# A two-layer encoder trunk: the residual sum stays in PSUM between the stages, and the router scales after it has multiplied

## The reference

```
x = x + mixer(rmsnorm(x, g1));  x = x + hier_moe(rmsnorm(x, g2), ...)        # two layers, then rmsnorm(x, ln_f)
rmsnorm(x, g) = x * rsqrt(mean(x*x) + EPS) * g
hier_moe: g_logits = h @ w_rg + b_rg (4 groups);  g_sel = argmax;  p_g = softmax(g_logits)[g_sel]
          e_logits = (h @ w_re + b_re) of the 8 experts of group g_sel;  top_p, top_j = top_k(softmax(e_logits), 2)
          gate = p_g * top_p / sum(top_p);  out = sum over the two experts of gate * ((silu(h@w_gate) * (h@w_up)) @ w_down)
```

## Time and profile before

| | |
|---|---|
| Three runs | 1380.62, 1379.73, 1380.55 us; median 1380.55 |
| Profiled execution: its time, its span | 1383.43 us, 1381.6 us |
| Granted clock of TensorE, mean | 0.86 |
| Busy: TensorE, weight load, VectorE, ScalarE, GpSimd | 1009.7, 738.1, 349.3, 266.8, 40.5 us |
| Read from memory | 455.58 MB |

### The profile page before, as it was taken

One profiled execution on the slowest core, in us unless ns is written; L12 is line 12 of the kernel. 1 busy time (PEld: TensorE's weight loads), 2 busy tenths in 40 slices (PEclk: granted clock), 3 DMA queues, 4 the chain that ended last, 5 costly groups with the idle time before them and its releaser, 6 DMA issues.

```text
span 1381.6 us, 28941 instructions
## 1 busy us (share of the span) xinstructions
PE 1009.7 (73%) x12804; PEld 738.1 (53%) x12804; DVE 349.3 (25%) x729; ACT 266.8 (19%) x551; POOL 40.5 (3%) x74
## 2 busy tenths in 40 slices
PE   5977987766757576765799999887676666757565
PEld 2944666535435353543577778675444444544443
DVE  4355332111111111110644545431111111102011
ACT  3444221000000000000453443511000000001001
POOL 2013200000000000000000000000000000000000
PEclk9975789869988787897899999989887988879886
DMA  9630059999999999999746635469999999999994
GB/s 322 240 122 0 1 223 389 426 426 424 428 427 426 425 428 426 426 425 412 263 153 226 226 130 178 156 250 427 424 426 426 427 425 427 426 426 426 427 426 180
DMA packets 55173, 458.45 MB, mean 332 GB/s; under 512 B 4960, under 2 KB 14240, under 8 KB 30352
## 3 DMA queue, kind: packets, MB, share of 16 engines
q1 hardware_dynamic: 53936, 452.96, 79.5%
q0 software_dynamic: 1120, 3.68, 0.9%
HBM read 455.58 MB, written 1.05 MB: 331 GB/s over the span
## 4 chain that ended last, share of the span: by engine, by line
DMA 54%; PE 38%; DVE 4%; issue 2%; POOL 1%; ACT 1%; DVEq 0%; SPq 0%; PEldq 0%; POOLq 0%; ACTq 0%
DMA ring<-in_w_down 21%; DMA ring<-in_w_up 16%; DMA ring<-in_w_gate 16%; PE wk L945 6%; PE wk L633 4%; PE wk L635 4%; PE wk L634 4%; PE wk L970 3%; PE wk L620 2%; PE acc L633 2%; PE acc L635 2%; PE acc L634 2%; PE acc L812 1%; PE wk L929 1%; DMA ring<-in_w_in_e 1%
## 5 line engine op out<-in xcount | busy, mean ns | idle before, releaser
L945 PE MATMUL wk<-ring,arena 128*32 128x128 f32 x8192 | 302.4, 309 | 156.5 <-DMA ring<-in_w_up 67.9
L945 PEld LDWEIGHTS wk<-ring,arena 128*32 128x32 f32 x8192 | 259.2, 125 | 209.0 <-DMA ring<-in_w_gate 87.5
L970 PE MATMUL wk<-ring,arena 128*32 128x256 f32 x2048 | 168.9, 484 | 123.6 <-DMA ring<-in_w_down 97.9
L970 PEld LDWEIGHTS wk<-ring,arena 128*32 128x32 f32 x2048 | 74.7, 132 | 200.0 <-issue 180.8
L1640 DVE TENSOR_TENSOR arena<-wk,arena 128x128 f32<-128x128 f32 x64 | 24.0, 375 | 434.7 <-ACT arena L1277 434.7
L1651 DVE COPY arena<-wk 32x256 f32<-32x256 f32 x128 | 54.3, 424 | 229.1 <-PE wk L970 228.3
L1284 ACT ACTIVATE arena<-wk 32x256 f32<-32x256 f32 x128 | 47.7, 373 | 305.4 <-PE wk L970 304.6
L1425 DVE TENSOR_TENSOR slot_parts<-ring,slot_parts 128x1024 fp32r<-128x1024 f32 (+1 forms) x78 | 97.2, 1301 | 31.5 <-ACT slot_parts L1136 31.0
L1277 ACT ACTIVATE arena<-wk 128x128 f32<-128x128 f32 x64 | 17.7, 277 | 450.5 <-PE wk L945 450.5
L1136 ACT ACTIVATE slot_parts<-ring 128x1024 fp32r<-128x1024 f32 (+1 forms) x78 | 81.8, 1114 | 49.2 <-PEq L1068 23.2
L929 PE MATMUL wk<-arena,xn 128*128 128x128 f32 x512 | 67.8, 296 | 19.6 <-issue 10.3
(11 more groups left out here) (267 smaller groups left out, 1067.7 us busy)
## 6 DMA issues: line engine op xcount, KB each, us to landing
ring<-in_w_gate SPq DMA_DIRECT2D x64, 2048.0 KB, 35.5
ring<-in_w_up SPq DMA_DIRECT2D x64, 2048.0 KB, 35.7
ring<-in_w_down SPq DMA_DIRECT2D x64, 2048.0 KB, 35.5
ring<-in_w_in_o SPq DMA_DIRECT2D x8, 2048.0 KB, 8.9
ring<-in_w_in_o SPq DMA_DIRECT2D x8, 1024.0 KB, 12.2
ring<-in_w_out_o SPq DMA_DIRECT2D x4, 2048.0 KB, 7.9
ring<-in_w_in_e SPq DMA_DIRECT2D x3, 2048.0 KB, 18.4
ring<-in_w_out_e SPq DMA_DIRECT2D x2, 2048.0 KB, 12.5
```

The costliest lines, as they stand in the source:

```text
L945: last = nc.tensor.matmul(wk[0][32 * j:32 * j + 32, part * P:(part + 1) * P], xe[:, k, :], w_[:, k, j * P:(j + 1) * P], start=(k == 0), st ...
L970: last = nc.tensor.matmul(wk[3][32 * j:32 * j + 32, 0:256], hidT[:, k, :], wd[:, k, j * 256:(j + 1) * 256], start=(k == 0), stop=(k == 3))
```

## The change

Four things are done.

1. **The sum stays in PSUM.** The four `acc` banks become one tensor `total`, which keeps the residual sum from the first output projection to the end. The copies to `x` and the seeds of both routers and of retention are gone; the four seeds of layer 0's output projection stay. Norms read `total`. EPS comes in as the root's bias, and a norm outside the routers squares 1024 columns in one instruction.
2. **Transposed unscaled.** In "ffn0" and "ffn1" VectorE multiplies the sum by the gain alone, as two instructions of 512 columns for each chunk, with no wait for the root. The reciprocal of the root multiplies the 36 logits later, and ScalarE scales `xn` by it in place (`xs`), for which the gather now waits.
3. **The chain of the two best** runs on all four groups at once (64 columns), with the group's choice placed between its steps; a ratio of two exponentials replaces the softmax over eight.
4. **In retention** the release of a weight part is attached to the first matmul of the part behind it, in seven of eight places, so that TensorE doesn't wait for itself.

```diff
-                seed_wide()
-
                 pe.wait_ge(dve_s, V.at(f"asg{l}"))
...
+                        pe.wait_ge(act_s, A.at(f"{e_}:xs1"))
                         pe.wait_ge(m["sel_ready"], it + 1)
...
             transposed_norm("mix1")
-            pe.wait_ge(dve_s, V.at("mix1:x1"))
-            pe.wait_ge(act_s, A.at("mix1:sa1"))
-            seed_wide()
             pe.wait_ge(dve_s, V.at("mix1:xl3"))
...
-                def used(name, hp):
-
-                    b, k = odd_use(name, hp)
-                    pe.wait_ge(odd_filled[b], i * 6 + (k + 1))
-                    pe.sem_inc(odd_used, 1)
...
-                        split_project(b[:, :], x_tok(c), lambda k: (hi[:, k, :], lo[:, k, :]), quarter, 4
-                                      ).then_inc(f, 1)
-                    used(f"{kind}1", hp)
+                        split_project(b[:, :], x_tok(c), lambda k: (hi[:, k, :], lo[:, k, :]), quarter, 4,
+                                      passed=(kind, c) == ("v", 0)).then_inc(f, 1)
...
+                            if (s, m_) == (0, 0):
+                                last.then_inc(odd_used, 1)
...
+                upper_squares(0)
+                lower_squares(0)
+                root(e_, 0, ms)
+                upper_squares(1)
+                turn_out(e_, 0)
+                turn_out(e_, 1)
+                lower_squares(1)
+                turn_out(e_, 2)
+                root(e_, 1, ms)
                 preload(ACT.Exp)
-                drain_xT(f"ffn{l}")
+                act.wait_ge(dve_s, V.at(f"{e_}:rs"))
+                for c in range(TC):
+                    act.wait_ge(pe_s, PE.at(f"{e_}:xT{2 * c + 1}"))
+                    nc.scalar.activation(xn[:, c, :, :], xn[:, c, :, :], ACT.Copy, scale=rstd[:, c:c + 1]
+                                         ).then_inc(act_s, A.done(f"{e_}:xs{c}"))
...
+                for c in range(TC):
+                    arrived(c)
+                    if c == 0:
+                        dve.wait_ge(gain_in[1], 16 * (l + 1))
+                    for hf, name in enumerate(("xa", "xn")):
+                        if hf:
+                            dve.wait_ge(act_s, A.at(f"{e_}:sb{c}"))
+                        tt(xn[:, c, :, 64 * hf:64 * hf + 64], by_eight(acc[2 * c + hf]),
+                           by_eight(gain[:, 1, hf * 512:(hf + 1) * 512]), ALU.mult
+                           ).then_inc(dve_s, V.done(f"{e_}:{name}{c}"))
+                dve.wait_ge(pe_s, PE.at(f"{e_}:xT3"))
+                nc.vector.tensor_copy(xnT[:, 4:8, P:2 * P], wk[3][:, :].rearrange("p (k t) -> p k t", k=4)
+                                      ).then_inc(dve_s, V.done(f"{e_}:xT3"))
+                dve.wait_ge(act_s, A.at(f"{e_}:std1"))
+                nc.vector.reciprocal(rstd, std).then_inc(dve_s, V.done(f"{e_}:rs"))
...
+                for c in range(TC):
+                    last = stt(lg[:, c, :], wk[0][:, c * 64:c * 64 + NR], rstd[:, c:c + 1], br[:, l, :],
+                               ALU.mult, ALU.add)
```

More of the change, by code:

```diff
@@ L552, in _ @@
             nc.gpsimd.memset(warm, 1.0)
+            nc.gpsimd.memset(eps, EPS)
             nc.gpsimd.memset(ones, 1.0).then_inc(ready, 1)
@@ new lines, in experts @@
+                tt(t4, gl, wide_of(gmax, GROUPS), ALU.subtract).then_inc(dve_s, V.done(f"gd{l}"))
+                link(stt(rest, one, -BIG, ea, ALU.mult, ALU.add))
+                link(nc.vector.reduce_max(best2, rest, AX.X))
+                tt(pair_gap, best2, best1, ALU.subtract).then_inc(dve_s, V.done(f"gap{l}"))
+                link(tt(two, rest, group_of(best2), ALU.is_equal))
+                link(tt(two, two, ar8, ALU.mult))
+                link(nc.vector.tensor_reduce(spot, two, AX.X, ALU.min))
```

221 lines of the change are left out of this document (121 added, 100 removed).

## The result

The changed kernel took 1365.72 us in the median of four runs (1363.68 to 1369.51), beside 1380.59 for the kernel before (four runs, 1379.73 to 1384.10). The ratio is 0.9891, 95% interval 0.9863 to 0.9918: 14.9 us faster. The profiled execution took 1365.70 us, its span is 1363.9, that is 17.7 us less than the span of before; 2.8 of them come from the execution of before that was profiled, which was that much above its median.

The account below looks back on a forecast made before the run. Loads bound the expert stages, so stream standstills before them and TensorE's gaps in retention count. 5.6 + 1.3 + 3.2 + 3.2 + 0.4 = 13.7 us gained, said as 1367.0 us; range of 8 in 10: 1361.5 to 1373.5.

Parts of the forecast that it names:

- Release of a part: Retention: TensorE no longer waits for its own last matmul at twelve places; 5.6 us gained, between 4.4 and 6.7.
- Norm mix1 with the start of retention: Before retention: passes without copies 1.95 us earlier, cold clock loses 1.0, warmer transposes return 0.4; sum 1.3 us gained.
- Layer 1's router: Norm and router in layer 1: 1.9 + 1.6 + 0.5 - 0.8 = 3.2 us gained, bounds 1.2 and 6.6.
- The logits' clock: Layer 1's router: shorter TensorE idle lets the clock fall half way through the logits; 1.6 us gained, bounds 0 and 3.0.
- Chain: Layer 1's router: VectorE's selection of the two best falls from 4.82 to 4.3 us, a gain of 0.5.
- Layer 0: Router of layer 0: earlier first release closes the stream's standstill; 3.2 us gained, bounds 2.5 and 3.3, no more possible.
- End: Last norm: ScalarE's last root no longer waits for VectorE's `EPS` instruction; 0.4 us gained.
- First norm: Start of the kernel: the norm hides behind the loads of the first weights; 0 gained.
- The waits only move: Retention: TensorE arrives earlier and waits for VectorE or a bank instead; gain 8.1, 1372.5 us; chance 0.07.
- Cold all along: Without seeds: half clock through transposes, logits and ranks, rising late in retention; gain 9.2, 1371.4 us; chance 0.15.
- PSUM strided is dear: Norms reading PSUM in strides: 512 columns take 2.2 us, twice the assumed time; gain 6.2, 1374.4 us; chance 0.08.
- slower: Norms: strided PSUM reads at 3.5 us for 512 columns eat all gains; 4.2 lost, 1384.8 us; chance 0.04.

Follow-up runs that it names:

- fill in front of retention: Changed kernel with TensorE's pause between norm mix1's transposes and the first retention matmul filled by matmuls of 256 columns of constants; 1364.04 us.
- old norm: Changed kernel with the norm before both routers in its former order, rows scaled by the root mean square ahead of the transposes; 1372.34 us.
- price measurement: Changed kernel with ten VectorE instructions of 512 columns, in order or in steps, added three times behind the last norm; one run, 1387.30 us.

## Why the prediction was right, and where its steps were off

**The sum.** 1367.0 was forecast, 1365.72 came, 14.9 us gained for 13.7. That is closer than its steps: two terms were too small by 3.3 us together, and a loss of 3.0 us at the end of layer 0 that it doesn't have made up for it. That loss is a state of the clock which eight of thirteen traces don't have (below), so this much of the closeness is luck.

**Release of a part: 5.6 us, bounds 4.4 to 6.7; measured 7.6.** The mechanism is right: twelve places count, the end of a round and the second head's transposes don't, and no wait took the place of those removed. The size is off, and above its bound. The bound took the starts around the waits, 3.35 us a round; measured the same way they are 3.2, so it had the scores' 0.65 us in it. What it lacked is the second matmul behind each wait, which comes 0.1 us late again (0.05 at the transposes); with what that adds, a round is 3.8 us. And 5.6 was taken between the two ends because each part's first matmul "will still pay a little": it pays nothing, the parts follow at 0.12 and 0.22 us. From before to after the stretch shows only 5.55, because the cold start takes its part.

**Norm mix1 with the start of retention: 1.3; measured 1.6.** VectorE's pieces start 8.13 us behind the combination for 11.06, which is 2.9 (forecast 1.95 by the copies and 0.4 by warmer transposes; the second transposes start 2.2 sooner and take 1.09 us for 1.97, at full clock). From the pieces' start to the last product of q and k it is 15.6 us for 14.3: 1.3 lost by the cold start, where 1.0 was forecast. The fill in front of retention recovers just that 1.3.

**Layer 1's router: 3.2; measured 4.5.** `xn` of chunk 1: forecast 1.9, the transposes start 2.0 sooner. The gain multiplication was put at 1.1 us and takes 1.11. The logits' clock: forecast "it falls half way", 1.6; it didn't fall within the logits, 3.2. That is the step that failed, by a little even against its bound of 3.0. The reason given, that the logits are light work since they never raised the clock, says nothing of when it falls: with 0.69 us of pause in front it fell 0.5 us behind them, with 2.38 (old norm) 0.9 us after their start. Chain: 0.5, measured 0.4 from before to after and 0.66 with the old chain put back. Ranks: 0.8 lost, measured 1.0. The gather lost another 0.3 (5.77 us for 5.46), and chunk 1's transposes gave 0.2. ScalarE's scaling of the rows (1.09 us a chunk) ended at 888.3 and was hidden by the selection.

**Layer 0: 3.2, "no more can be won"; measured 3.2.** The dip is gone, the release moves by 1.5 us between kernels without setting the layer's time, and the old norm, 3.2 us later at the release, brought the dip back.

**End: 0.4; measured 0.5.** The root no longer waits: from the end of the combination to the end of the span it is 6.2 us for 6.7. The stage as a whole gained under 0.2 us, because two other things in it nearly cancel: the combination took 3.70 us for 5.24 by the clock, and the last product's weights landed about 2 us later behind the issue of their load (that product starts 38.05 us behind it for 36.07). Why they landed later is open.

**First norm: 0.** The trace shows 0.3 us there, and -0.3 to 1.3 over all kernels.

**The clock at places that the change leaves alone** was no part of the prediction. The profiled pair has +2.8 us in attention and -3.0 at the end of layer 0 (down projection and combination at half clock). Of the thirteen traces of kernels derived from the change, the combination of layer 0 took 3.7 us in eight and 5.5 to 5.9 in five. That is the scatter of the medians, and a difference of 1 to 2 us between two kernels here is only to be trusted where a stage shows it.

**The rivals.** "The waits only move" is refuted by the kernel with the waits put back. "Cold all along" is refuted for the logits and holds for retention's start. "PSUM strided is dear" and "slower" rested on one read, and the price measurement ends both: 0.69 us in steps as in order. The rule of the Trainium skill, "SBUF — State Buffer", section "Door 1: The DMA port swizzle", that leaving a 16-byte line of SBUF costs, agrees with the trace (0.38 us more for 512 columns in steps of 32 bytes). For PSUM's 8-byte line that section speaks of matmuls only; to carry it over to VectorE was the prediction's own step, and for VectorE reading fp32 it costs nothing that these rows show.

## What to carry to other kernels

A chain between two stretches of dense matmuls was paid twice here: its own length, and the half clock of what follows; so shorten first the pause that stands in front of much TensorE work, and read the granted clock behind it. A wait of TensorE for its own last matmul cost more than the idle time that the profile shows beside it (0.55 us ahead of a projection for 0.29 shown, 0.75 ahead of the scores for 0.50): hang the release on the next instruction. Where a transfer stands still, work out how long: past that point an engine's gain is worth nothing, as in layer 0.

## What the runs showed of the hardware

- VectorE reads fp32 from PSUM in steps of 32 bytes at the price of order (0.691 and 0.688 us for 512 columns), while one SBUF operand in such steps makes it 1.065; two of them (1.075) or a stepped output (1.076) make it hardly dearer.
- 32 matmuls of 36 columns in a row ran at full clock throughout, 3.66 us, when the transposes ahead of them had started within 0.7 us of other work, and at half throughout, 6.88 us, when those started behind 2.7 us of idling. At full, the clock fell soon after them: 0.5 us behind their end in the changed kernel, and as far behind it with a fill running there.
- A fill is no certain means: the same ten matmul records took 4.01 us at half clock in one kernel, and the clock was up again for the ranks; in two others they took 2.40 us at full clock, a pause of 2.22 us followed, and it fell at the ranks.
- A release by a wait for TensorE's own last matmul cost 0.45 to 0.65 us at the start of the next part and 0.05 to 0.10 more at its second matmul; attached to the next part's first matmul it cost nothing.
